# Modulation vectors formed by VectorE as row dot products during the input projections, where TensorE formed them in blocks of their own

## The reference

```python
def trunk_layer(x, cvec, p, ml_state, ctx_cache, angles):
    mod = (jax.nn.silu(cvec) @ p['ada_w'] + p['ada_b'])[:, None, :]
    sh1, sc1, g1, sh2, sc2, g2 = jnp.split(mod, 6, axis=-1)
    h = rmsnorm(x, p['norm1_g']) * (1 + sc1) + sh1
    (mq, mk, mv, mo, i_f, f_f, i_b, f_b, cu, cv, cq, ckv, kr) = split_cols(h @ p['w_in'])
    ...                      # mLSTM, spatial gating and latent attention on these columns
    x = x + g1 * (mixed @ p['w_out'])
    h = rmsnorm(x, p['norm2_g']) * (1 + sc2) + sh2
    return x + g2 * peer_layer(h, ...)      # product-key retrieval of experts, then the experts
```

## Time and profile before

| | us |
|---|---|
| median of 3 runs | 4160.45 (4154.36 to 4161.46) |
| the profiled execution's own time | 4159.9 |
| span of its profile | 4157.9 |
| second block, first modulation | about 10.8 to 110 |
| projections of layer 0 | about 111 to 265.4 |
| projections of layer 1 | about 2128 to 2285.1 |

### The profile page before, as it was taken

How to read it: one execution, slowest core, us unless ns; L and a number is a source line. 1 busy time by engine, 2 the same in 40 slices (tenths; PEclk the granted TensorE clock), 3 DMA queues, 4 the chain that set the end, 5 groups by cost and what they waited for, 6 DMA issues and landing times. The chain is left out here.

```text
span 4157.9 us, 60980 instructions
## 1 busy us (share of the span) xinstructions
PE 3841.7 (92%) x20790; PEld 3269.5 (79%) x20790; DVE 3236.9 (78%) x6660; ACT 1433.2 (34%) x2566; POOL 2177.0 (52%) x1554
## 2 busy tenths in 40 slices
PE   8879998978999999999969889897889999999996
PEld 1776688637899999999959657891789999999996
DVE  0224557998999999999950557599989999999997
ACT  1331223147333333333333223311853333333332
POOL 0210012387777777777722000226967777777773
PEclk9875999989999999999979589998999999999998
DMA  6311001445999999999931110125489999999995
GB/s 269 112 46 43 1 21 63 181 165 211 405 405 406 405 401 394 403 401 397 398 116 42 36 41 21 43 82 203 203 332 405 405 405 402 392 404 402 400 400 222
DMA packets 300883, 1047.86 MB, mean 252 GB/s; under 512 B 30032, under 2 KB 82000, under 8 KB 290480
## 3 DMA queue, kind: packets, MB, share of 16 engines
q0 software_dynamic: 147456, 536.94, 32.7%
q1 hardware_dynamic: 153264, 508.85, 32.0%
HBM read 992.11 MB, written 53.56 MB: 251 GB/s over the span
## 5 line engine op out<-in xcount | busy, mean ns | idle before, releaser
L1530 POOL DMA_INDIRECT picked_rows<-in_u_rows,chosen x512 | 788.6, 1540 | 315.8 <-DVE dots_now L1806 183.2
L1530 POOL DMA_INDIRECT picked_rows<-in_v_rows,chosen x512 | 809.0, 1580 | 261.2 <-DVE y L1814 144.7
L1703 PE MATMUL ps<-hd_hi,u_hi 128*128 128x384 f32 x2048 | 698.6, 341 | 19.9 <-DVE a_lo L1796 11.2
L1703 PE MATMUL ps<-hd_hi,u_lo 128*128 128x384 f32 x2048 | 696.6, 340 | 0.0
L1703 PE MATMUL ps<-hd_lo,u_hi 128*128 128x384 f32 x2048 | 695.6, 340 | 0.0
L1814 DVE SCALAR_TENSOR_TENSOR y<-picked_rows,dots_now,y 128x1024 f32<-128x1024 f32 x512 | 644.0, 1279 | 0.0
L1806 DVE CUSTOM_DVE_ANT_0 picked_rows<-picked_rows,h2rows 128x1024 f32<-128x1024 f32 x512 | 614.1, 1218 | 0.0
L1714 PE MATMUL ps<-v_hi,a_hi 128*128 128x512 f32 x1536 | 479.0, 393 | 0.0
L1714 PE MATMUL ps<-v_hi,a_lo 128*128 128x512 f32 x1536 | 475.2, 390 | 0.0
L1714 PE MATMUL ps<-v_lo,a_hi 128*128 128x512 f32 x1536 | 473.2, 389 | 0.0
L1742 ACT ACTIVATE v_hi<-v_raw 128x1024 fp32r<-128x1024 f32 x256 | 271.8, 1062 | 509.1 <-PE ps L1714 508.8
(11 more groups left out here) (304 smaller groups left out, 7198.1 us busy)
## 6 DMA issues: line engine op xcount, KB each, us to landing
u_raw<-in_u SPq DMA_DIRECT2D x256, 512.0 KB
v_raw<-in_v SPq DMA_DIRECT2D x256, 512.0 KB
gates_dram<-gmat SPq DMA_DIRECT2D x12, 4096.0 KB, 11.5
gt<-gates_dram SPq DMA_DIRECT2D x64, 768.0 KB
wq<-in_ada_w SPq DMA_DIRECT2D x16, 2048.0 KB, 7.9
wring<-in_ada_w SPq DMA_DIRECT2D x12, 2048.0 KB, 7.9
w_raw<-in_w_in SPq DMA_DIRECT2D x18, 1024.0 KB, 4.8
wq<-in_wq SPq DMA_DIRECT2D x8, 2048.0 KB, 7.9
```

What stands on the lines that cost most here:

```text
L1530: pool.indirect_dma_start(picked_rows[:, n % RING, :], None, a[table], bass.IndirectOffsetOnAxis(ap=chosen[:, m % GT, m // GT:m // GT + 1] ...
L1703: ins = pe.matmul(ps[:, b % 2, 0:TD], (u_hi, u_lo)[wl][:, b % 2, k, :], (hd_hi, hd_lo)[hl][:, k, :], start=(k == 0 and n == 0), stop=(k == ...
```

## The change

TensorE no longer forms modulation. The weights are laid out turned, so that one part of 128 output columns is a 512 KB tile with an output on each partition and its 1024 weights along the row. The silu of each conditioning vector is spread over all partitions (`c_rows`), and one fused multiply-and-sum of VectorE (`modulate`, L220) gives a column of 128 results. A part takes two of these, one for each conditioning.

- The two blocks at the start become one. It forms only sh1 and sc1 of layer 0: 16 parts, 32 dot products, from an 8 MB buffer that is loaded in six pieces. The 2.5 MB of `x` are loaded between the fourth and the fifth.
- `project` forms 48 parts (96 dot products) on VectorE after `normalise`: gates, then sh2 and sc2 of this layer, then sh1 and sc1 of the next. They come through a ring of three 512 KB tiles, each loaded again when its part has been used. Gates are turned by one TensorE transpose ahead of c = 5, copied by ScalarE, and written to `g_dram`; `gate1` and `gate2` are loaded from there at the end. The additions of L557 are gone.
- The low parts of `w_in` for c = 2 to 8 are subtracted by VectorE, after parts 7, 12, 17, 22, 27, 32 and 37, and no longer by GpSimd.
- `retrieve` no longer forms modulation.

```diff
+    PARTS = 6 * KD
+    LOW_W = [7 + 5 * i for i in range(7)]
+    MOD_SLOTS = 3
...
+    def modulate(dve, m, rows, ring, junk, j, first=0):
...
+        n = 2 * (j - first)
+        for v in range(2):
+            if n + v >= len(junk):
+                dve.wait_ge(m["used"], n + v - len(junk) + 1)
+            dve.tensor_tensor_reduce(junk[(n + v) % len(junk)], ring[(j - first) % len(ring)], rows[:, v, :], 1.0, 0.0,
+                                     ALU.mult, ALU.add, column(j, v)).then_inc(m["used"], 1)
...
+    FIRST = (0, 1, 2, 4, 8, 12, 2 * KD)
...
-            modulation_loads(sp, mod_sems, ring, xn[0:2, :, 0:512], a["ada_w"][DEPTH - 1], a["ada_bT"][DEPTH - 1],
-                             lambda j: None)
-
-        @block.tensor
-        def _(pe):
-            modulation_products(pe, mod_sems, ring, xn[0:2, :, 0:512])
+            sp.dma_start(c_rows[:, :, :], a["c"].partition_broadcast(P)).then_inc(c_load0, 16)
+            for i in range(len(FIRST) - 1):
+                lo, hi = FIRST[i], FIRST[i + 1]
+                sp.dma_start(first_ring[:, lo:hi, :], a["ada"][DEPTH - 1, 4 * KD + lo:4 * KD + hi].rearrange("j p d -> p j d")
+                             ).then_inc(first_mod["slot"][i], 16)
...
+                if i == 3:
+                    sp.dma_start(x[:, :, :], a["x"].rearrange("(t p) d -> p t d", p=P)).then_inc(x_load, 16)
...
+            act.activation(c_rows[:, :, :], c_rows[:, :, :], ACT.Silu).then_inc(silu, 1)
...
+                def load_part(j):
+                    if j >= MOD_SLOTS:
+                        sp.wait_ge(mod["used"], 2 * (j - MOD_SLOTS) + 2)
+                    sp.dma_start(mod_ring[:, j % MOD_SLOTS, :], a["ada"][l, j]).then_inc(mod["slot"][j % MOD_SLOTS], 16)
...
+                load_w(0)
+                sp.dma_start(c_rows[:, :, :].rearrange("p a b -> p (a b)"), c_dram.rearrange("a b -> (a b)").partition_broadcast(P)).then_inc(c_in, 16)
+                load_w(1)
...
             def _(pool):
-                for c in range(9):
+                for c in range(2):
...
+                def part(j):
+                    dve.wait_ge(mod["slot"][j % MOD_SLOTS], 16 * (j // MOD_SLOTS + 1))
+                    modulate(dve, mod, c_rows, ring, junk, j)
+                    if j in LOW_W:
+                        c = LOW_W.index(j) + 2
+                        dve.wait_ge(w_high, c + 1)
+                        dve.wait_ge(w_split, c)
+                        dve.tensor_tensor(w_lo[:, c % 2, :, :], w_raw[:, c % 2, :, :], w_hi[:, c % 2, :, :],
+                                          ALU.subtract).then_inc(w_split, 1)
...
+                for j in range(4 * KD, 6 * KD):
+                    part(j)
+                dve.wait_ge(mod["used"], 2 * PARTS)
+                finish_modulation(dve, link, 1, normT[:, 0, :])
+                finish_modulation(dve, link, 0, normT[:, 1, :])
...
-                modulation_loads(sp, mod_sems, ring2, rows2, a["ada_w"][l], a["ada_bT"][l], slot_free)
...
-                modulation_products(pe, mod_sems, ring2, rows2)
```

More of the change, by code:

```diff
@@ L137, in normalise @@
             first()
-            if "mod" in n:
-                act.wait_ge(n["mod"], 4)
             for t in range(NT):
@@ L400, in build_program @@
     s1.close()
-    mod_sems = modulation_sems("mod", K.sem)
-    first_squares = nc.alloc_semaphore("first_squares")
-    ring = [wring[:, i, :, :] for i in range(3)]
+    load = K.sem("first_loads")
+    x_load = K.sem("x_load")
+    c_load0 = K.sem("c_load0")
+    c_stored = K.sem("c_stored")
+    pre = K.sem("first_constants")
+    silu = K.sem("silu_ready")
+    first_chain = K.sem("first_chain")
+    first_squares = K.sem("first_squares")
+    FIRST = (0, 1, 2, 4, 8, 12, 2 * KD)
+    first_mod = dict(slot=[K.sem(f"first_slot{i}") for i in range(len(FIRST) - 1)], used=K.sem("first_used"))
     with nc.Block() as block:
@@ new lines, in _ @@
+            sp.wait_ge(silu, 1)
+            sp.dma_start(c_dram, c_rows[0:1, :, :].rearrange("p a b -> p (a b)")).then_inc(c_stored, 16)
+            sp.wait_ge(load, 48)
+            sp.wait_ge(c_stored, 16)
+        @block.vector
+        def _(dve):
+            link = chain_of(dve, first_chain)
+            dve.memset(eps_col[:, :], EPS).then_inc(pre, 1)
+            dve.memset(one_col[:, :], 1.0).then_inc(pre, 1)
+            dve.wait_ge(pre, 2)
+            dve.wait_ge(silu, 1)
+            for j in range(2 * KD):
+                if j in FIRST:
+                    dve.wait_ge(first_mod["slot"][FIRST.index(j)], 16)
+                modulate(dve, first_mod, c_rows, [first_ring[:, i, :] for i in range(2 * KD)],
+                         [mod_junk[:, :], xn[:, 1, :]], 4 * KD + j, 4 * KD)
+            dve.wait_ge(first_mod["used"], 4 * KD)
+            dve.wait_ge(load, 48)
+            finish_modulation(dve, link, 0, normT[:, 1, :])
@@ L555, in _ @@
-                for gate, bias in ((gate1, cqT), (gate2, ckvT)):
-                    both = gate[:, :, :].rearrange("p v (a b) -> p v a b", a=2)
-                    dve.tensor_tensor(both, both, bias[:, :, 0:512].unsqueeze(1).to_broadcast([P, 2, 2, 512]), ALU.add)
+                normalise(None, dve, None, 0, dict(n1, link=link))
+                ring = [mod_ring[:, i, :] for i in range(MOD_SLOTS)]
+                junk = [mod_junk[:, :], xn[:, 1, :]]
+                def part(j):
[7 more added lines that the diff above has]
+                                          ALU.subtract).then_inc(w_split, 1)
```

153 lines of the change are left out of this document (89 added, 64 removed).

## The result

| | median | runs |
|---|---|---|
| before | 4160.17 us | 4154.36 to 4161.46, 4 runs |
| changed | 4123.84 us | 4122.85 to 4126.17, 4 runs |

The ratio is 0.9916, with a 95% interval from 0.9899 to 0.9933: the change makes the kernel 36 us or 0.9% faster. The forecast was 4102, 58 us faster, with a range of 4092 to 4126. So the sign is right and the time is in the range, close to its upper end, and more than a third of the expected gain isn't there.

The account below looks back on a forecast made before the run. It took TensorE to bound the first modulation and projections, with the retrieval's modulation in a hole. Terms -63.0 + 2.8 + 2.1 - 0.2 = -58.3 us turned 4159.9 into 4101.6, or 4102.2 for the median; 8-in-10 range 4092 to 4126.

Parts of the forecast that it names:

- no overlap: Rival at start and projections: dot products chain at 1.30 us each, giving 4137; chance 0.15 shared with a milder ring delay.
- mild starving: Rival in the projections' ring: half a us lost on every part, giving 4150; chance 0.15 shared with non-overlapping dot products.
- a slower start: Rival at the start: pieces at 321 GB/s and late spread vectors, layer 0 at 57 not 48, 4111; chance 0.14.
- The start: Before layer 0: VectorE sets the end with 32 dot products; layer 0 begins at 48.0 instead of 110.96, -63.0 us.
- The wait for the fifth piece: In the start: VectorE is ready at 25.9 us, the piece of parts 8 to 11 lands at 27.7, so 1.8 us.
- The rule of the Trainium skill that the prediction weighed: Every dot product: halved throughput for two non-bf16 SBUF sources, 1.1 us more each, over 180 us slower; chance 0.01.
- The head of the projections: Start of each layer's projections: `c_rows` delays the second weight block 2.6 us, mostly caught; +0.6 us a layer.
- The body: Projections after `normalise`: the end passes from TensorE to VectorE, 126.4 us of work; +2.8 us layer 0, +2.1 layer 1.
- Does VectorE wait for weights?: Projections' ring of tiles: tiles land some 3.9 us after being asked for, against 4.6 us allowed; no wait.
- the hard end of a rival: Projections' ring: at 6.6 us latency each layer loses 32 us, 4166; chance 0.02 for 4150 to 4168, 0.05 above.
- TensorE and the low parts: Projections: VectorE's low parts come every 13.7 us against TensorE's need every 14.4, so TensorE doesn't wait.
- The retrieval: Removing 88 us of TensorE modulation lies in a hole and saves 0; rival with a few us gained, 4092, chance 0.04.

Follow-up runs that it names:

- four places: The changed kernel with four places instead of three for the modulation tiles in the projections, the added one lying in `gate2`; 4111.50 us, ratio 0.9884.

## Why the prediction was right or wrong

The time, 4123.84, lies in the range of 8 in 10 by 2 us. It doesn't lie in the 4096 to 4108 that had 0.60, but in the band of the rivals (no overlap, or mild starving) that had 0.15. The range reached so far up for those rivals and a slower start, and the loss that filled it is a wait that the main sum put at nothing. The start, which is nearly all of the gain, came as forecast; that the range holds the time is in part luck.

**The start: right.** Forecast 48.0, measured 48.34. The spread vectors' silu ended 0.6 us sooner than the sum had it. The wait for the fifth piece was forecast at 1.8 us and is 2.01, and the dot product is the one of the earlier trace rows. In this timeline the next starts 1.15 us after it, as in the earlier trace rows:

```profile
7.12 1.23 DVE L220 CUSTOM_DVE_ANT_0 mod_junk<-first_ring,c_rows 128x1024 f32<-128x1024 f32 x1 [6.21 <-ACT c_rows L385]
8.27 0.08 DVE L220 DVE_READ_ACCUMULATOR2_ANT modT<- 128x1 f32 x1
...
27.55 1.23 DVE L220 CUSTOM_DVE_ANT_0 mod_junk<-first_ring,c_rows 128x1024 f32<-128x1024 f32 x1 [2.01 <-DMA first_ring<-in_ada]
```

The rival without overlap (1.30 us each) falls with this, and so does the slower start. The rule of the Trainium skill that the prediction weighed ("Vector Engine (DVE) Microarchitecture Reference", section 7) would have made each 1.1 us longer; these rows don't bear it out. The page names one instruction form, and no row shows whether the dot product is of it.

**The head of the projections: right in layer 0, too small in layer 1.** Forecast +0.6; layer 0 shows 0 (free at 78.48, 30.1 us after the stage began, 30.2 before), layer 1 2.6. The step (the second block moves by 2.6 us, and most of this is caught) is right for what the order costs in layer 0 and in layer 1 of the changed kernel, about 0.6 us each. Left out was that the loads of layer 1 don't start when they did: the first block is issued 2.4 us later after the mark than before, and its copy begins 2.15 us later. That accounts for the rest of the 2.6. Its cause stays open.

**The body: right as work, wrong as waits.** From the end of `normalise` to VectorE's end the sum was 126.4 us. It is 134.2 in the changed kernel (78.48 to 212.72), and 127.7 with four places. So the sum of the work is off by 1.3 us, and the failed step is the one under "Does VectorE wait for weights?": "A 512 KB load should land in 4.8 - 1.3 = 3.5 us ... so the tile lands some 3.9 us after it is asked for. I take no wait." Measured: 4.4 us in the median, and 7.0 and 6.1 us for the tiles behind the weight blocks at 99.9 and 130.0. This step took the landing time of a load that had the queue to itself, 4.8 us for 1 MB, for a stretch in which the queue carries 223 GB/s instead of 69, and in which the same 1 MB takes 6.5 us. The row for another 512 KB load, 6.6 us for `wuk`, was in the text, but only as the hard end of a rival. The Trainium skill, "DMA: Bandwidth & Descriptors", section "Anatomy of one DMA — SWDGE (gpsimd) path", has 2.0 us plus bytes at 436 GB/s, which would be 3.2 us for a tile, for another kind of queue. The quickest tile here took 3.3, the median 4.4, the slowest 7.1: the page's figure is near the quickest, and a ring has to cover the slowest.

What it cost: the waits are 6.4 and 7.6 us, and four places bring the two stages down by 7.0 and 9.0, 16 us together. (In layer 1 of that kernel VectorE was free 31.8 us after the mark and not 32.4, so 0.6 of these 16 are the head's.) The projections were missed by 18.8 us: 14.0 are the waits, some 2 the head of layer 1, and the rest the sum of the work. It is the rival of the mild starving, but with a price of 0.15 us on every part (14.0 us over 96) where that rival had 0.5.

**TensorE and the low parts: right.** TensorE is busy 124.9 us against 123.7 after `normalise`, and waits for `w_lo` 0.2 us in layer 0 and 0.8 in layer 1. ScalarE's last copy of the products ends 1.0 us later in the stage than before in the changed kernel, and no later with four places (154.3 us after the stage began, 154.4 before).

**The retrieval: right.** Taking 88 us of TensorE out changed the stages by -1.7 and -0.3 us, no more than they differ between the eleven traces with the change (617.2 to 621.0 and 617.3 to 619.1 us). TensorE now waits for the whole of it, and the turning of the picked keys still begins when VectorE lets it (compare):

```profile
819.40 0.45 PE L1341 MATMUL ps<-ident,pqT 128*128 128x128 f32 x1 [91.60 <-DVEq L1480]
```

**What stays open.** Gates and experts are 3.7 and 1.2 us longer than in the one trace of before, though nothing was changed there. Over the eleven traces with the change they take 1245.3 to 1249.5 us in layer 0 and 1241.7 to 1246.0 in layer 1, and before lies below both spans (1244.7, 1241.2). A small real cost of 1 to 4 us in all can't be told from the spread, and none of the runs was made to find it. Of the 3.7 us, 1.0 is the later table load at the turn of the layer (4.6 us after the last clearing, 3.6 before). TensorE's clock doesn't explain it. Its mean over the span falls from 0.939 to 0.917, since in the retrieval it is 0.50, the level of 1.2 GHz, where TensorE now has nothing to do (761.6 to 816.6 us), and was 1.00. But in the last 15 us ahead of this stage it is 0.50 in both kernels, and over its first 20 us 0.61 in both. Nor is it settled why SP starts later after the turn of the layer, and why an issue there takes up to 2.7 us.

## What to carry to other kernels

Size a ring by the slowest landing in the company that the loads will have, not by the median of a load alone. With n places and t us of work per tile, (n - 1) x t must reach it (here 4.6 us were too few and 6.9 enough), and smaller tiles make this worse, since the landing time shrank less than the work (4.4 to 3.0 us against a half). Where a change moves work to another engine and at the same time out of the way, price the two apart: here nearly all of the gain came from forming two vectors instead of six ahead of the first layer, and the engine, with its loads, was worth 4 us in the other direction. Compare stages by a mark, and ask whether the mark itself moved: in layer 1 SP was ahead of it before and behind it after, and that was most of what looked like the cost of one load's place. Before a helper engine is given half of a subtraction that runs beside VectorE's two-input operations, look whether they exclude each other.

## What the runs showed of the hardware

- A load of 512 KB on SP's queue lands after 3.3 to 7.1 us at 223 GB/s, 4.4 in the median; behind loads of 1 MB that took 7.5 and 7.1 us it took 7.0 and 6.1, and behind one that took 5.1 it took 4.1. One of 256 KB, in the same place, takes 3.0 in the median. The 1 MB load itself goes from 4.8 us to 6.5, and to 7.2 when more tiles are in flight.
- A multiply-and-sum of VectorE over 1024 float32 columns takes 1.22 us, over 512 columns 0.69. So some 0.16 us are fixed (an estimate, 2 x 0.69 - 1.22). The next one starts 1.15 us after it.
- GpSimd's subtraction of two SBUF operands and VectorE's operation with two SBUF sources exclude each other: beside it 1.22 us become 5.63, and 2.29 become 6.71.
- The second load that SP issues after the turn of the layer held it for 0.47 to 2.67 us in ten traces with the change and 1.76 before it; a tile's issue takes 0.33.
